# Moving expert rows through a DRAM table with indirect DMA in a one-core decoder trunk

## The reference, cut to what matters

```python
logits = (hf @ w_router)                       # hf: (256, 1024), 8 experts
topv, topi = lax.top_k(logits, 2)
wts = jax.nn.softmax(topv, axis=-1)
gate = jnp.sum(jax.nn.one_hot(topi, 8) * wts[..., None], axis=1)
for e in range(8):                             # D_FF_EXPERT = 3584
    out = out + gate[:, e:e + 1] * ((silu(hf @ wg[e]) * (hf @ wu[e])) @ wd[e])
```

## Time and profile before

| | |
|---|---|
| median of 3 runs | 1574.69 us (1574.67 to 1574.76) |
| the profiled execution's own time | 1574.66 us |
| its span in the trace | 1572.9 us |
| TensorE busy | 1550.6 us, 99% of the span |
| VectorE, ScalarE, GpSimd busy | 492.3, 404.7, 33.3 us |
| DMA traffic | 478.88 MB, mean 304 GB/s |
| visit 0 starts, the last visit's products end | 720.4 us, 1557.3 us |

### The profile page before, as it was taken

How to read it: one execution, slowest core, us unless ns; L and a number is a source line. 1 busy time by engine, 2 the same in 40 slices (tenths; PEclk the granted TensorE clock), 3 DMA queues, 4 the chain that set the end, 5 groups by cost and what they waited for, 6 DMA issues and landing times. The chain is left out here.

```text
span 1572.9 us, 34011 instructions
## 1 busy us (share of the span) xinstructions
PE 1550.6 (99%) x15650; PEld 1070.5 (68%) x15650; DVE 492.3 (31%) x547; ACT 404.7 (26%) x470; POOL 33.3 (2%) x119
## 2 busy tenths in 40 slices
PE   8999999999999999999999999999999999999996
PEld 8999898998989998985454444444454544534544
DVE  5554656455456646544001010010010100100102
ACT  5444455443345444542001000010010100100101
POOL 1000000000000000103000000000000000000000
PEclk9999999999999999999999999999999999999998
DMA  9655643556465555777999999999999999999992
GB/s 352 192 178 172 220 161 109 168 175 226 157 211 173 176 188 188 279 289 285 357 409 364 421 419 418 421 418 420 420 376 421 419 418 421 419 419 414 392 421 94
DMA packets 115252, 478.88 MB, mean 304 GB/s; under 512 B 8772, under 2 KB 13988, under 8 KB 86436
## 3 DMA queue, kind: packets, MB, share of 16 engines
q1 hardware_dynamic: 115108, 476.69, 78.7%
HBM read 475.61 MB, written 1.05 MB: 303 GB/s over the span
## 5 line engine op out<-in xcount | busy, mean ns | idle before, releaser
L1630 PE MATMUL ps<-unit,h_slots 128*32 128x384 f32 (+1 forms) x5376 | 513.1, 539 | 5.0 <-issue 5.0
L1630 PEld LDWEIGHTS ps<-unit,h_slots 128*32 128x32 f32 x5376 | 183.4, 110 | 312.9 <-issue 310.4
L920 DVE TENSOR_TENSOR wlo<-raw,whi 128x2048 fp32r<-128x2048 f32 (+1 forms) x116 | 259.0, 2236 | 208.2 <-ACT whi L597 208.1
L1323 PE MATMUL ps<-a_hi,whi 128*128 128x256 f32 x992 | 281.4, 284 | 0.0
L1323 PE MATMUL ps<-a_hi,wlo 128*128 128x256 f32 x992 | 280.7, 283 | 0.0
L1323 PE MATMUL ps<-a_lo,whi 128*128 128x256 f32 x992 | 280.7, 283 | 0.0
L597 ACT ACTIVATE whi<-raw 128x2048 fp32r<-128x2048 f32 (+1 forms) x116 | 216.8, 1870 | 162.1 <-PE ps L1323 104.6
L1323 PEld LDWEIGHTS ps<-a_lo,whi 128*128 128x128 f32 x992 | 190.4, 192 | 0.1
L1323 PEld LDWEIGHTS ps<-a_hi,whi 128*128 128x128 f32 x992 | 190.4, 192 | 0.1
L1323 PEld LDWEIGHTS ps<-a_hi,wlo 128*128 128x128 f32 x992 | 190.4, 192 | 0.0
L1655 PE MATMUL ps<-unit,actT 128*32 128x256 f32 x2688 | 149.6, 379 | 0.0
(11 more groups left out here) (247 smaller groups left out, 1415.8 us busy)
## 6 DMA issues: line engine op xcount, KB each, us to landing
unit<-in_w_e_gate SPq DMA_DIRECT2D x64, 1024.0 KB, 16.8
unit<-in_w_e_up SPq DMA_DIRECT2D x64, 1024.0 KB, 18.3
unit<-in_w_e_down SPq DMA_DIRECT2D x64, 1024.0 KB, 15.5
unit<-in_w_e_gate SPq DMA_DIRECT2D x64, 768.0 KB, 13.8
unit<-in_w_e_up SPq DMA_DIRECT2D x64, 768.0 KB, 12.9
unit<-in_w_e_down SPq DMA_DIRECT2D x32, 1536.0 KB, 17.6
raw<-in_w_in SPq DMA_DIRECT2D x32, 1024.0 KB, 5.6
raw<-in_w_xk SPq DMA_DIRECT2D x8, 1024.0 KB, 5.2
```

Source lines behind the costliest of these rows:

```text
L920: dve.tensor_tensor(wlo[n % SPL][:, 0:size], raw[n % RAW][:, 0:size], whi[n % SPL][:, 0:size].bitcast(F32), ALU.subtract).then_inc(s["lo_r ...
L1323: ins = pe.matmul(o[:, d, :], w[wi][:, k, d * P:(d + 1) * P], xs[xi][:, k0 + k, :], start=first and d % 2 == 0, stop=last, skip_group_chec ...
L1630: ins = pe.matmul(ps[q * QP:(q + 1) * QP, b0 + h, 0:n], he[:, k, h * QP:(h + 1) * QP], w[:, q * n:(q + 1) * n], start=k == 0, stop=k == KD ...
```

## The change

A table of 2304 rows of 4 KB (`slot_rows_dram`: 24 visit numbers with 96 slots each) is added in DRAM.

- SyncE writes zeros to all of it (18 transfers of 512 KB and one of 256 KB) between the first loads of the program's first part.
- GpSimd, behind its last table, works out the table row of each of a token's two picks in about twenty-five more small operations and writes the 256 normalised rows to these places, with four indirect DMAs of 128 rows (512 KB) each.
- For each visit from 1 on SyncE loads the visit's 96 or 64 rows (`load_rows`, ahead of its unit 0), and TensorE turns them into `he` with eight transposes (`rows_t`) in place of `gather`.
- The outputs of visits 0 to 6 are copied out of PSUM as before, but no longer weighted, split, scattered and added. SyncE stores them to the visit's rows of the table (`store_rows`, ahead of unit 25 of the next visit).
- In the last visit, SyncE waits until unit 25 has been used and all stores have landed, and loads `g_final`. GpSimd waits for `g_final` and fetches each token's two output rows with four indirect DMAs, 512 KB each. VectorE adds them, weighted, to `x` (`add_picked`) before it leaves the block. The last visit's own outputs are scattered as before; `slot_t` runs only in it, after step 25.

The core of the diff:

```diff
+                def load_rows(v, n_groups):
+                    sp.wait_ge(s["h_stored"], 16 * 2 * NT)
+                    n = n_groups * QP
+                    src = rows_visit[bass.ds(v, 1), 0:n, :].rearrange("v r d -> r (v d)")
+                    sp.dma_start(hrow[0:n, :], src).then_inc(s["h_loaded"], 16)
+                def store_rows(v, n_groups):
+                    for done in ("yact_done", "ydve_done"):
+                        sp.wait_ge(s[done], every(v, 1, 0))
+                    n = n_groups * QP
+                    dst = rows_visit[bass.ds(v - 1, 1), 0:n, :].rearrange("v r d -> r (v d)")
+                    sp.dma_start(dst, y32[0:n, :]).then_inc(s["y_stored"], 16)
...
                     for i in range(BODY):
                         ring_wait(i, v)
+                        if i == 0:
+                            load_rows(v, n_groups)
+                        elif i == Y_AFTER:
+                            store_rows(v, after_groups)
                         load_expert_unit(i, e)
...
-                sp.wait_ge(s["unit_used"], every(last, BODY, U0 + TURN + 1))
+                sp.wait_ge(s["unit_used"], every(last, BODY, U0 + PICKED_UNIT + 1))
+                sp.wait_ge(s["y_stored"], every(last, 16, 16))
                 sp.dma_start(gfin[:], a["g_final"].rearrange("(a d) -> a d", a=1).broadcast_to([P, D])
                              ).then_inc(s["gfin_loaded"], 16)
...
+                pool.tensor_copy(h_row[:], row_of[:]).then_inc(s["row_done"], 1)
+                pool.wait_ge(s["row_done"], 1)
+                for c in range(2):
+                    for t in range(NT):
+                        pool.indirect_dma_start(slot_rows_dram[:, :], bass.IndirectOffsetOnAxis(ap=h_row[:, c, t:t + 1], axis=0),
+                                                hg[:, t, :], None).then_inc(s["h_stored"], 16)
...
+                pool.wait_ge(s["gfin_loaded"], 16)
+                pool.tensor_copy(y_row[:], row_of[:]).then_inc(s["row_done"], 1)
+                pool.wait_ge(s["row_done"], 2)
+                for c in range(2):
+                    for t in range(NT):
+                        pool.indirect_dma_start(picked[:, c, t, :], None, slot_rows_dram[:, :],
+                                                bass.IndirectOffsetOnAxis(ap=y_row[:, c, t:t + 1], axis=0)
+                                                ).then_inc(s["picked_loaded"], 16)
...
+                def add_picked():
+                    dve.wait_ge(s["row_done"], 2)
+                    dve.wait_ge(s["picked_loaded"], 16 * 2 * NT)
+                    for c in range(2):
+                        for t in range(NT):
+                            last_add = dve.scalar_tensor_tensor(out=x[:, t, :], in0=picked[:, c, t, :], scalar=pick_gate[:, c, t:t + 1],
+                                                                in1=x[:, t, :], op0=ALU.mult, op1=ALU.add)
+                        link(last_add)
...
+                def rows_t(v, n_groups):
+                    pe.wait_ge(s["h_loaded"], every(v, 16, 0))
+                    n = n_groups * QP
+                    for k in range(KD):
+                        o = bank(3 + k // 4)[:, (k % 4) * P:(k % 4) * P + n]
+                        ins = pe.transpose(o, hrow[0:n, k * P:(k + 1) * P], ident[0:n, 0:n])
+                        if k % 4 == 3:
+                            ins.then_inc(s["g_done"], 1)
...
                     for i in range(BODY):
+                        if i == ST_AFTER + 1 and not more:
+                            pe.wait_ge(s["st_ready"], 1)
                         (down if order[i][0] == "down" else gate_up)(i, v, n_groups)
-                        if i == SCATTER_AFTER:
-                            scatter(v)
-                        if i == ST_AFTER:
+                        if i == ST_AFTER and not more:
                             slot_t(v)
...
                         if more and i == GATHER_AFTER:
-                            gather(every(v, 1, 2))
+                            rows_t(every(v, 1, 1), next_groups)
```

More of the change, by code:

```diff
@@ L166, in trunk @@
     rs = place("rsum_s", [P, DEPTH, NH, NT], F32)
-    place("act_tok1", [P, C], F32)
+    zeros = place("act_tok1", [P, C], F32)
     assert at["top"] <= nc.sbuf_usable_end, (at["top"], nc.sbuf_usable_end)
@@ L242, in trunk @@
     ST = moe("sel_slot", [P, SEQ], F32R, late)
+    visit_no, visit_of, own_row, over_row = [moe(f"row_part{i}", [P, NE], F32, late) for i in range(4)]
+    row_in, row_over = [moe(f"row_of_pick{i}", [P, NT, NE], F32, late) for i in range(2)]
+    row_of = moe("row_of", [P, 2, NT], F32, late)
+    before_last = moe("before_last", [P, 2, NT], F32, late)
+    pick_gate = moe("gate_of_pick", [P, 2, NT], F32, late)
+    h_row = moe("h_row_index", [P, 2, NT], I32, late)
+    y_row = moe("y_row_index", [P, 2, NT], I32, late)
     yh = place("y_hi", [P, D], F32R, place_of["mem_hi"])
@@ L247, in trunk @@
     gfin = place("g_final_rows", [P, D], F32, ring)
+    picked = place("y_of_pick", [P, 2, NT, D], F32, ring + 6144)
+    PICKED_UNIT = 25
     order = []
@@ L392, in _ @@
                     load_unit(u)
+                    if u < 4 + COLS * CAP // P:
+                        sp.dma_start(blocks[u - 4], zeros[:].unsqueeze(1).to_broadcast([P, 2, C])).then_inc(s["rows_zeroed"], 16)
                 sp.wait_ge(s["merged_ready"], 2 * DEPTH)
@@ new lines, in _ @@
+                link(pool.tensor_tensor(row_in[:], pos[:], over_t(own_row), ALU.add))
+                link(pool.tensor_tensor(row_over[:], row_over[:], row_in[:], ALU.subtract))
+                link(pool.tensor_scalar(within[:], above[:], 0.0, None, ALU.is_gt))
+                link(pool.tensor_tensor(row_over[:], row_over[:], within[:], ALU.mult))
+                link(pool.tensor_tensor(row_in[:], row_in[:], row_over[:], ALU.add))
+                for c, hot in enumerate((rt[0], rt[3])):
+                    link(pool.tensor_tensor(row_over[:], row_in[:], hot[:], ALU.mult))
+                    for n in (4, 2):
+                        link(pool.tensor_tensor(row_over[:, :, 0:n], row_over[:, :, 0:n], row_over[:, :, n:2 * n], ALU.add))
+                    link(pool.tensor_tensor(row_of[:, c, :], row_over[:, :, 0], row_over[:, :, 1], ALU.add))
@@ L881, in visit @@
                 def visit(v, n_groups=SG, after_groups=SG):
-                    y_hi(v, after_groups)
+                    if not isinstance(v, int) or v:
+                        y_out(v, after_groups)
                     for g in range(NG2):
@@ L1222, in y_lo, with slot_rows @@
                     ins.then_inc(s["ydve_done"], 1)
[L1223 to L1237, removed]
+                def slot_rows():
+                    dve.wait_ge(s["ts_done"], 1)
                     dve.tensor_copy(ST[:], bank(5)[:, 0:SEQ])
@@ L1647, in down @@
                     pe.wait_ge(s["actT_ready"], every(v, NG2, g + 1))
+                    if g == 0 and part == 0:
+                        for done in ("yact_done", "ydve_done"):
+                            pe.wait_ge(s[done], every(v, 1, 0))
                     unit_landed(i, v)
@@ L1659, in down @@
                     ins.then_inc(s["unit_used"], 1)
[L1661 to L1670, removed]
                 def slot_t(v):
                     pe.wait_ge(s["gatev_ready"], 1)
+                    pe.wait_ge(s["last_s_ready"], 1)
                     for t in range(NT):
```

100 lines of the change are left out of this document (66 added, 34 removed).

## The result

The changed kernel takes 1596.50 us (median of 4 runs, 1594.12 to 1599.84) against 1574.72 us, 1.0139 times as long (95% interval 1.0121 to 1.0158). It is 1.4% slower, and outside the range of 1570 to 1585. The profiled execution took 1596.37 us, 20.4 more than forecast; its span is 1594.7 us.

The account below looks back on a forecast made before the run. TensorE bounded the kernel before, with loads only 14 us ahead; the loads would become the bound. Last unit 1543.3, g_final 1544.5, fetches 1553.2, additions 1558.6, last block 1558.9, 1.3 us later: 1574.66 + 1.3 = 1576.0 us, range 1570 to 1585.

Parts of the forecast that it names:

- TensorE's savings: Scatter, slot_t and gather work dropped from TensorE: 6.25 us for a visit, 45.8 us over the layer.
- The hidden parts: Zeros, GpSimd's row numbers and SyncE's waits, covered by other work: costed at nothing, perhaps a microsecond lost at first loads.
- the series of links in the forecast: At the end: last unit, g_final, four fetches, additions, border; last block begins at 1558.9 in place of 1557.6.
- signs of being wrong: Last unit before 1538 or after 1550, SyncE standing at stores, first part ending after 720 us, fetches over 10 us.
- how much the loads let through: In the expert layer, loads become the bound, last unit lands at 1543.3, and TensorE's 46 us shrink to 11.
- The row transfers: Six row loads and seven stores, 4.59 MB on SyncE's queue: 13.2 us, bounds 10.9 and 15.6.
- The thin slices: Two slices of 376 and 392 GB/s ending visits 3 and 6: 4.0 us recovered, bounds 0 and 6.7.
- Visit 1's step 20: Its load, issued as visit 0 ends 6.25 us earlier, lands at 838.7 in place of 845.0.
- The fetch: At the end, GpSimd's four indirect DMAs after g_final: 8.4 us, bounds 6.4 and 10.4, landing at 1553.2.
- the second one: Rival: fetches go one after another, or row transfers cost a full tile each: 1578 to 1584.4 us, 40%.

Follow-up runs that it names:

- full_loads: Changed kernel with each row load taking 128 rows to 128 partitions (512 KB) in place of 96 or 64: 1582.34 us, ratio 1.0051.
- bare: Changed kernel with row loads and output stores cut to 64 bytes of each row, without indirect row stores, fetch and additions of fetched rows: 1556.54 us, ratio 0.9881.
- tiny_loads: Changed kernel with each of the seven row loads cut to the first 64 bytes of its rows: 1575.62 us, ratio 1.0006.
- outs_early: Changed kernel with only outputs going through the table, rows made by gather as before the change, and g_final issued on ScalarE's queue: 1568.80 us, ratio 0.9963.
- act_gfin: Changed kernel with g_final issued by ScalarE on its own queue in the last visit, so the fetch runs beside the last units: 1589.77 us, ratio 1.0099.

## Why the prediction was wrong

**What held.** TensorE's savings: visit 0 ends at 832.98, forecast 833.1. It also started 0.5 us later than before, so it is 6.9 us shorter, forecast 6.25. The eight transposes are the 0.71 us here (for a visit of 64 slots), 0.97 forecast.

```profile
828.43 0.71 PE L1774 MATMUL ps<-ident,h_slot_rows 64*128 64x64 f32 x8
829.07 4.09 PE L1751 MATMUL ps<-unit,actT_end 128*32 128x256 f32 x72
832.98 1.47 PE L1723 MATMUL ps<-unit,h_slots 128*32 128x512 f32 x12
```

The hidden parts: the zeros cost 0.5 us, since visit 0 starts at 720.9 and not at 720.4. GpSimd issues the first indirect store at 742.34, forecast 742, and SyncE the first row load only at 780.75. SyncE never stands at the stores: from 720 us to the last unit all its waits are for TensorE. The bound moved from TensorE to the loads, and the end became the series of links in the forecast: `g_final` 1.2 us behind the last unit, additions and border 5.6 us, forecast 5.7. Of its own signs of being wrong, the landing of the last unit (after 1550) came true clearly, and the end of the first part (720.9, not 720) by less than 1 us.

**The step that failed** is how much the loads let through. The last unit was forecast for 1543.3 us and landed at 1561.9. The 18.6 us are three terms:

- *The row transfers*, 13.2 us forecast (bounds 10.9 and 15.6) and 24.1 us measured (719.5 - 695.4): +10.9. The seven stores cost 5.0 us, about their bytes, and the six row loads 18.7 us. My upper bound took for granted that a tile on fewer partitions costs at most what a full one does. By full_loads it costs about three times a full one (3.1 against 1.1 us), although it moves fewer bytes.
- *The thin slices*, 4.0 us forecast and none recovered: +4.0. I took the two slices of 376 and 392 GB/s for time by which all later landings were late. bare has no such slices (its windows move 418 GB/s from 833 to 1450 us) and its load stretch is the same, and in the kernel before the units of visit 4 landed almost evenly through the thin stretch (44 units from 1116.4 to 1220.9, none late by more than 1.2 us). Engines did stand idle there: the packets of SyncE's queue in the whole run hold all the bytes that it issued (476.7 MB), so no transfer is missing from the record. The slice of 1140.4 to 1179.7 us in 40 pieces, in the kernel before (share of the DMA engines in tenths, then the rate):

```profile
DMA  9999989996899999985493999999999999999999
GB/s 425 409 417 425 342 309 384 367 254 229 369 379 388 404 406 425 413 369 225 192 256 117 392 409 400 434 411 406 419 469 400 413 419 463 407 392 400 419 432 438
```

Around 1160 us, where visit 3 ends, the share falls to 0.5 and below in three of four pieces. But a unit lands when its slowest part does, and it is likely that only engines that had run ahead of the others stood idle; the trace does not name the engines, so this is argued. The end of the changed kernel shows how far they can be apart (share 0.49 from 1550 to 1560 us, and units landing as fast as ever).

- *Visit 1's step 20*, forecast for 838.7 and landed at 842.4: +3.7. It was issued at 833.22 as worked out, but the unit ahead of it landed only at 839.9, and before the change at 840.1 against an issue of step 20 at 839.57: there is a queue ahead of it now. In tiny_loads it lands at 839.0. The difference of 3.4 us is there from visit 1's unit 0 on (793.6 against 790.2), so it comes from visit 1's own row load, which I had called covered because it is issued early. The wait for it was covered, but not the time that it takes on the queue. (bare, also with a tiny load, has step 20 at 840.9, so between 1.5 and 3.4 us of the 3.7 are due to the load.)

**The fetch** took 10.6 us from `g_final` to the last landing, forecast 8.7: +1.9, at the upper end of my bounds (0.3 + 10.4). The first fetch is issued 0.9 us behind `g_final`, not 0.3, and the four take 9.7 us, not 8.4. The fetches neither go one behind the other nor side by side: they are issued every 1.3 us, and the four land 4.4, 5.3, 5.9 and 5.8 us after their issues. By the Trainium skill, page "DMA: Bandwidth & Descriptors", section "Anatomy of one DMA — SWDGE (gpsimd) path", fetches one after another would take 12.8 us and overlapped ones 6.8, an estimate; the trace has 9.7 us from the first issue to the last landing, between the two.

Together 18.6 + 1.9 - 0.1 = 20.4 us, the whole miss. The split of the 18.6 us over its three terms holds to about 2 us, because each rests on single landings; the sum does not depend on it. The rival that came true is the second one, "the row transfers cost a full tile each", by its direction only: its upper end was 1584.4. The rule of the Trainium skill on the 16 ports, page "Advanced Engine Details and Errata", section "DMA Bandwidth Details", spoke for a price above the bytes. The trace agrees in part: the price does hang on the partitions, but only for loads, and it is more than the idle ports explain (3.1 us for a tile that costs 1.1 us on all partitions). Why loads are hit and stores are not stays open: the traces do not tell which DMA engine writes which partition.

## What to carry to other kernels

When the DMA queue is nearly full, look at the shape of each small load that is put into it, and not only at its bytes: spread over all 128 partitions it cost its bytes here, on 96, 64 or 32 partitions three to four times as much, paid by the big loads beside it. Work that another engine did for nothing is dear to move onto a queue that is full: once the scatters were gone and the loads set the pace, `gather` cost TensorE 3 us per visit more that nobody waited for (outs_early), while its replacement cost the queue 3 us per visit that everybody waited for. What stands at the very end in series (a small load, then a fetch, then additions) should start on another queue while the last big loads run; that was worth 7 to 8 us here.

## What the runs showed of the hardware

- A load of 384 or 256 KB to 96 or 64 partitions cost 3.1 us in a stream of 1 MB loads, and one of 128 KB to 32 partitions 1.2 us; one of 512 KB to 128 partitions cost 1.1 us. Around the loads to 96 or 64 partitions the engine time for a MB was 42 to 48 us (40 to 41 with 32 partitions, 38 to 39 with 128). Stores of 384 or 256 KB from 96 or 64 partitions delayed the unit behind them by 0.9 or 0.6 us, their bytes.
- Behind a deep queue the 16 DMA engines do not finish together: in the changed kernel their share was 0.49 (205 GB/s) from 1550 to 1560 us, while units of 1.5 MB went on landing every 3.7 us.
- An indirect DMA of 128 rows of 4 KB occupies GpSimd for 0.95 to 1.08 us, and the next is issued 1.3 us after it. Alone, the first landed 4.4 us after its issue; beside the unit loads (act_gfin) the four took 10.1 to 19.8 us each.
- A transfer on ScalarE's queue did not wait for the 30 us of loads outstanding on SyncE's: 8.0 us to landing and not 30.9.
